# Row sums on VectorE for two parts of the conditioning, with their weights behind the first projection's

## The chip, the cores and the metric

The kernel runs on one core of a Trainium2 chip. The metric is the device time of one execution in microseconds (us), the median of several runs. Engines are named as the profile names them: PE (TensorE, matrix products; PEld its weight loads), DVE (VectorE), ACT (ScalarE), POOL (GpSimd), SP (SyncE, which here only issues DMAs). A time with a start is measured from the start of the span.

## What is computed

One layer for 256 tokens of width 1024. A conditioning vector c is multiplied with a 1024 x 6144 matrix w_ada; the six pieces of 1024 are shifts, scales and gates used in different places. Then two mixers (gated DeltaNet and forgetting attention, "FoX") share one input projection, are gated and merged, and a top-4-of-32 expert network follows.

```python
mod = (c @ w_ada[l] + b_ada[l]).reshape(B, N_MOD, D)
sh1, sc1, gt1, sh2, sc2, gt2 = [mod[:, i, None, :] for i in range(N_MOD)]
h = rms_norm(x, g_norm1[l]) * (1.0 + sc1) + sh1
proj = h @ w_in[l]
# split: dn_qkv, dn_z, dn_b, dn_a, fx_qkv, fx_f, gate_a, gate_b
y_a = o_a.reshape(B, S, DN_W) @ w_o_delta[l]      # DeltaNet branch
y_b = o_b.reshape(B, S, FOX_W) @ w_o_fox[l]       # FoX branch
merged = sigmoid(gate_a) * y_a + sigmoid(gate_b) * y_b
x = x + gt1 * (merged @ w_out[l])
h2 = rms_norm(x, g_norm2[l]) * (1.0 + sc2) + sh2
x = x + gt2 * moe_ffn(h2, ...)
```

All is float32. The change touches c @ w_ada, the order in which weights arrive, and the place of y_b = o_b @ w_o_fox.

## The kernel before

Every engine has its own written-out instruction stream; semaphores join them. SBUF has a ring of 20 slots of 8 KB per partition (1 MB each). Until the experts start, slots 0 to 7 carry a stream of 54 units of 1 MB (list UNITS): unit n goes into slot n mod 8, and SP issues its DMA once unit n - 8 has been used, in order. The order is ada0 (8 units), dn (6), fqk (4), fv (2), z (2), ada1 (8), gates (8), ada2 (8), wo_fox (2), wo_delta (2), w_out (4). The units ada0, ada1 and ada2 are the three parts of w_ada, 2048 columns wide, one unit for each block of 128 rows (k = 0 to 7). Units dn, fqk, fv, z and gates are 256 columns of w_in each. A unit of w_ada is one run of 8 KB per partition, a unit of w_in eight runs of 1 KB.

**Conditioning.** ada(part, b) on PE does four matmuls for each k: block k of c, repeated over 32 columns, is the stationary operand, 512 columns of the unit are the moving one, and the result is summed over k in bank b of PSUM. take_mod_rows on DVE (L1369) copies the bank to mod_rows; mod_transposes on PE (L513 to L520) turns the rows to columns; take_mod on DVE adds the bias. Part 0 is needed for h. Part 1 (gt1, sh2) is done on PE after the products of keys and queries, part 2 (sc2, gt2) inside the DeltaNet recurrence, in three pieces that fill PE's waits (between_state, between_vnew).

**Projection in three passes.** Most units of w_in are split into a rounded half and a rest (list SPLIT): ACT writes the rounded half w_hi to one of three buffers (split_hi, L1096), POOL subtracts and writes the rest w_lo in place over the unit (L1789, two instructions of 128 x 1024 for each unit), and PE takes three products. ACT splits two units ahead of PE; the first two gates units are split after ACT has taken the second z (take, L1130).

**Order of PE around the change.** dn 0 to 5; the small projection; fqk 0 to 2; cumulative sums of the log gates (they need g8 from DVE, L1401 to L1421, a chain of short instructions that also waits for ACT); fqk3, fv, z; chunk_pairs; ada(1) and its transposes; gates 0; six levels of the triangular inverse with half a gates unit between each two steps; the recurrence over four chunks; four blocks of the FoX branch (out_branch with wf and obT, two columns of 128 each); the normalised DeltaNet output transposed (oT_ps), four blocks of its branch; the output projection. DVE's chain after chunk_pairs is: L1482 (scores times decay), L1488 (mask of level 0), L1493, L1488 (level 1), L1499, L1501, and then take_mod_rows(1).

**What follows.** SP issues the first experts' weights on oT_ps, yb_ps, ya_ps, merged_ready and out_ps, as slots come free; then 32 experts stream 12 MB each through the 20 slots.

Of the kernel before, what the change touches and what calls it, by code (L numbers as in the profile page):

```python
# [15 lines left out]
ALU = mybir.AluOpType  # L16
# [3 lines left out]
P = 128  # L20
# [20 lines left out]
def layer_kernel(nc, x, c, w_ada, b_ada, g_norm1, w_in, conv_w, a_log, dt_bias, g_onorm, b_fgate,  # L41
# [3 lines left out]
    KD = D // P  # L45
# [26 lines left out]
    with ExitStack() as ctx:  # L72
# [208 lines left out]
        UNIT_AT = {(name, i): n for n, (name, i, _) in enumerate(UNITS)}  # L281

# [203 lines left out]
        def _(pe):  # L486
# [36 lines left out]
            pe.wait_ge(S("cb_ready"), 1)  # L523
            ada(0, 4, range(2))
# [169 lines left out]
            ada(1, 5)  # L694
# [61 lines left out]
            for h in range(H):  # L756
# [8 lines left out]
            pe.wait_ge(S("hT_whole"), 1)  # L765
            between_state = {1: lambda: project("gates", LEVELS, (1,)), 2: lambda: project("gates", LEVELS + 1, (1,)),
                             3: lambda: ada(2, 6, range(3, 6))}
            between_vnew = {0: lambda: project("gates", LEVELS, (0,)), 1: lambda: project("gates", LEVELS + 1, (0,)),
                            2: lambda: ada(2, 6, range(3)), 3: lambda: ada(2, 6, range(6, KD))}
# [30 lines left out]

            wf = [unit_arrived(pe, "wo_fox", u).rearrange("p (k n) -> p k n", k=2) for u in range(2)]

            def out_branch(w, o, b, g, sem):
                for m in (2 * g, 2 * g + 1):
                    for k in range(H):
                        last = mm(bank(b, (m % 2) * T, T), w[k // 2][:, k % 2, m * P:(m + 1) * P], o[:, k, :],
                                  k == 0, k == H - 1)
                last.then_inc(S(sem), 1)

            pe.wait_ge(S("proj_taken"), nproj[0] - 6)  # L810
            for g in range(4):
                if g >= 2:
                    pe.wait_ge(S("yb_taken"), g - 1)
                out_branch(wf, obT, g % 2, g, "yb_ps")
                if g == 0:
                    mod_transposes(2, 6)
                if g == 1:

                    pe.wait_ge(S("on_ready"), 1)
                    for h in range(H):  # L820
                        for t in range(TT):
                            last = pe.transpose(bank((2, 7)[h // 2], (h % 2) * T + t * P, P), o_sb[:, t, h, :], ident)
                    last.then_inc(S("oT_ps"), 1)
# [231 lines left out]
        def _(act):  # L1055
# [27 lines left out]
            def split_hi(n, m):  # L1083
# [7 lines left out]
                elif prev is not None:  # L1091
                    if m == 0 and name != "fv" and SPLIT[prev][0] != "fv":
                        act.wait_ge(S("half_used"), prev + 1)
                    else:
                        act.wait_ge(S("unit_used"), UNIT_AT[SPLIT[prev]] + 1)
# [17 lines left out]
            def take(name, u):  # L1113
# [9 lines left out]
                act.wait_ge(S("unit_used"), UNIT_AT[(name, u)] + 1)  # L1123
# [206 lines left out]
        def _(dve):  # L1330
# [36 lines left out]
            def take_mod_rows(part, b):  # L1367
                dve.wait_ge(S("unit_used"), UNIT_AT[(f"ada{part}", KD - 1)] + 1)
# [15 lines left out]

            for u in range(6):
                dve.wait_ge(S("unit_used"), UNIT_AT[("dn", u)] + 1)
# [10 lines left out]
                last.then_inc(S("conv_ready"), 1)  # L1397
            dve.wait_ge(S("conv_ready"), 6)
# [9 lines left out]
            STT(ab8, y8, -1.0, y8, ALU.mult, ALU.max).then_inc(S("y8_ready"), 1)  # L1408

# [7 lines left out]
            link(STT(y8, y8, 0.0, g8, ALU.max, ALU.subtract))  # L1417
            dve.wait_ge(S("l8_ready"), 1)
# [18 lines left out]
            last.then_inc(S("rowF_taken"), 1)  # L1437
            dve.wait_ge(S("rowF_taken"), 1)
# [68 lines left out]
            for s in range(1, LEVELS):  # L1507
# [19 lines left out]
                if s == 2:  # L1527
# [6 lines left out]
                    TS(fmax, fmax, -1.0, None, ALU.mult).then_inc(S("fox_max_ready"), 1)  # L1534
                if s == 3:
# [5 lines left out]

            dve.wait_ge(S("M_ready"), LEVELS - 1)
# [3 lines left out]
            for n in range(NCH):  # L1546
                t, r = n // 2, (n % 2) * CH
                rows = slice(r, r + CH)
                if n > 0:
                    dve.wait_ge(S("ws_ps"), n)  # L1550
                    TTn(vnew[rows, t], u_sb[rows, t], ps[rows, 2, :].rearrange("p (h n) -> p h n", h=H),
                        ALU.subtract).then_inc(S("vnew_ready"), 1)
                if n < NCH - 1:
# [7 lines left out]
                    last.then_inc(S("state_ready"), 1)  # L1561
                    dve.wait_ge(S("state_ready"), n + 1)
# [7 lines left out]
            take_yb(0)  # L1570
            take_mod(2, 6)
# [7 lines left out]
            take_yb(1)  # L1579
# [5 lines left out]
            take_yb(2)  # L1585
# [4 lines left out]
            take_yb(3)  # L1590
# [191 lines left out]
        def _(pool):  # L1782
# [9 lines left out]
            pool.wait_ge(S("unit_used"), UNIT_AT[SPLIT[-1]] + 1)  # L1792
# [67 lines left out]
```

## Time and profile before

| | us |
|---|---|
| median of 3 runs (lowest, highest) | 1234.74 (1232.75, 1236.36) |
| the profiled execution's own time | 1238.22 |
| its span, first to last instruction | 1236.4 |
| PE busy | 1140.0 (92%) |
| DVE busy | 318.3 (26%) |
| ACT busy | 185.4 (15%) |
| POOL busy | 106.0 (9%) |
| mean granted TensorE clock | 0.98 of full speed |
| moved by DMA | 464.71 MB, mean 376 GB/s |

How to read the profile: a row of a timeline gives start, duration, engine, line of the kernel and operation, result and operands, shape, how many instructions are merged in it (x), and in brackets how long the engine had been idle and who released it. The duration of an instruction includes time in which it has been issued and is held up. A float32 matmul shows as two instructions. All matmuls go through a helper, so they have line 488 and are told apart by their operands and shapes. "Issue" names a wait for which the profile shows no releaser. The granted clock is the share of TensorE's full speed (2.4 GHz) that it was given; 0.5 is 1.2 GHz.

### The profile page before, as it was taken

The numbers are of one execution on the slowest core, as the hardware profiler recorded it, in microseconds if no ns is written. First come the engines' busy times: TensorE is split into PE (matmuls) and PEld (weight loads), VectorE is DVE, ScalarE is ACT, GpSimd is POOL, SyncE is SP. The second block draws the span as 40 slices with busy tenths as digits, with TensorE's granted clock in tenths as the row PEclk, the third lists the DMA queues.
The fourth block names the chain that finished last, engine by engine and source line by source line (L and its number), as shares of the span: only waits on it lengthen the run. The fifth ranks groups of instructions, "written<-read, shape, count | busy, mean of one in ns | idle before, by whom it ended". The sixth has DMA issues, their size and how long they took to land.

```text
span 1236.4 us, 15127 instructions
## 1 busy us (share of the span) xinstructions
PE 1140.0 (92%) x6307; PEld 588.1 (48%) x6307; DVE 318.3 (26%) x674; ACT 185.4 (15%) x317; POOL 106.0 (9%) x50
## 2 busy tenths in 40 slices
PE   4999999999999999998989998989999999989896
PEld 2999799678543334333334333333433334333332
DVE  1632553131332222212122212121221222122102
ACT  2475344101310000000001000000000010000002
POOL 0764344010000000000000000000000000000000
PEclk9998999999999999999989999999999999999999
DMA  9972773498899999999999999999999999999995
GB/s 351 337 226 93 242 234 103 146 420 335 329 404 426 428 428 428 429 428 429 428 429 428 428 429 428 429 429 428 429 428 429 428 429 428 429 428 428 429 427 246
DMA packets 62559, 464.71 MB, mean 376 GB/s; under 512 B 8469, under 2 KB 31130, under 8 KB 34618
## 3 DMA queue, kind: packets, MB, share of 16 engines
q1 hardware_dynamic: 61688, 462.92, 91.2%
q10 hardware_dynamic: 786, 1.14, 0.3%
q8 instruction: 26, 0.43, 0.1%
q0 software_dynamic: 48, 0.13, 0.0%
q14 instruction: 11, 0.09, 0.0%
HBM read 463.13 MB, written 1.05 MB: 375 GB/s over the span
## 4 chain that ended last, share of the span: by engine, by line
PE 65%; DMA 28%; issue 2%; ACT 2%; DVE 1%; ACTq 0%; POOL 0%; SPq 0%; DVEq 0%
PE ps L488 63%; DMA ring<-in_w_down_dram 16%; DMA ring<-in_w_gate_up_dram 6%; DMA kept<-in_w_down_dram 4%; DMA ring<-in_w_in_dram 1%; PE ps L939 1%; ACT kept L1290 1%; DMA ring<-in_g_onorm_dram 1%; PE ps L971 0%; ACT w_hi L1096 0%; PE ps L496 0%; POOL w_lo L1789 0%; ACT ring L1079 0%; DVE kept L1419 0%; ACT ring L1134 0%
## 5 line engine op out<-in xcount | busy, mean ns | idle before, releaser
L488 PE MATMUL ps<-ring,kept 128*64 128x512 f32 (+1 forms) x3040 | 656.2, 598 | 35.0 <-DMA ring<-in_w_down_dram 19.0
L488 PEld LDWEIGHTS ps<-ring,kept 128*64 128x64 f32 (+1 forms) x3040 | 211.7, 137 | 451.7 <-issue 399.2
L488 PE MATMUL ps<-kept 128*128 128x128 f32 (+4 forms) x984 | 195.7, 415 | 8.3 <-ACT kept L1290 3.3
L488 PEld LDWEIGHTS ps<-kept 128*128 128x128 f32 (+2 forms) x984 | 110.5, 179 | 95.8 <-issue 83.1
L1286 ACT ACTIVATE kept<-kept 128x512 f32<-128x512 f32 x32 | 20.1, 629 | 729.5 <-DVE kept L1691 729.5
L1691 DVE TENSOR_SCALAR kept<-ps 128x512 f32<-128x512 f32 x32 | 22.1, 692 | 384.6 <-PE ps L488 384.6
L1713 DVE TENSOR_TENSOR kept<-ps,kept 64x512 f32<-64x512 f32 x64 | 44.1, 689 | 296.0 <-PE ps L488 295.0
L1789 POOL TENSOR_TENSOR w_lo<-ring,w_hi 128x1024 fp32r<-128x1024 f32 x38 | 91.9, 2434 | 110.3 <-ACT w_hi L1096 110.2
L488 PE MATMUL ps<-hT_hi,w_hi 128*128 128x256 f32 x272 | 78.5, 289 | 0.6 <-POOL w_lo L1789 0.6
L488 PE MATMUL ps<-ring 64*64 64x64 f32 (+6 forms) x784 | 76.0, 272 | 2.9 <-issue 2.9
L488 PE MATMUL ps<-hT_lo,w_hi 128*128 128x256 f32 x272 | 76.8, 282 | 0.0
L488 PE MATMUL ps<-hT_hi,w_lo 128*128 128x256 f32 x272 | 76.8, 282 | 0.0
L488 PEld LDWEIGHTS ps<-ring 64*64 64x64 f32 (+3 forms) x784 | 66.5, 160 | 12.9 <-issue 6.8
L488 PE MATMUL ps<-kept,ring 128*128 128x256 f32 (+1 forms) x252 | 56.2, 380 | 4.5 <-DMA ring<-in_w_in_dram 2.5
L488 PEld LDWEIGHTS ps<-kept,ring 128*128 128x128 f32 x252 | 47.2, 196 | 12.1 <-issue 3.3
L488 PEld LDWEIGHTS ps<-hT_hi,w_hi 128*128 128x128 f32 x272 | 52.1, 191 | 1.3 <-issue 0.8
L488 PEld LDWEIGHTS ps<-hT_lo,w_hi 128*128 128x128 f32 x272 | 52.0, 191 | 0.1
L488 PEld LDWEIGHTS ps<-hT_hi,w_lo 128*128 128x128 f32 x272 | 52.0, 191 | 0.0
L1096 ACT ACTIVATE w_hi<-ring 128x1024 fp32r<-128x1024 f32 x38 | 39.2, 1053 | 49.5 <-PE ps L488 37.5
L939 PE MATMUL ps<-kept 128*128 128x128 f32 x128 | 21.7, 292 | 22.6 <-issue 22.6
L939 PEld LDWEIGHTS ps<-kept 128*128 128x128 f32 x128 | 19.1, 206 | 33.4 <-issue 29.6
L1290 ACT ACTIVATE kept<-ps 128x512 f32<-128x512 f32 x32 | 19.1, 597 | 85.7 <-PE ps L939 85.7
(229 smaller groups left out, 516.4 us busy)
## 6 DMA issues: line engine op xcount, KB each, us to landing
ring<-in_w_gate_up_dram SPq DMA_DIRECT2D x127, 2048.0 KB, 27.8
ring<-in_w_down_dram SPq DMA_DIRECT2D x47, 2048.0 KB, 23.5
kept<-in_w_down_dram SPq DMA_DIRECT2D x16, 2048.0 KB, 25.1
ring<-in_w_ada_dram SPq DMA_DIRECT2D x24, 1024.0 KB, 5.4
ring<-in_w_in_dram SPq DMA_DIRECT2D x22, 1024.0 KB, 11.5
ring<-in_w_out_dram SPq DMA_DIRECT2D x4, 1024.0 KB, 16.2
ring<-in_w_o_fox_dram SPq DMA_DIRECT2D x2, 1024.0 KB, 9.8
ring<-in_w_o_delta_dram SPq DMA_DIRECT2D x2, 1024.0 KB, 12.7
```

The costliest lines, as they stand in the source:

```text
L488: return pe.matmul(dst, lhsT, rhs, start=start, stop=stop, skip_group_check=True)
L939: last = pe.transpose(bank(7, kk * P, P), fours[:, kk, :], ident)
L1096: A(hi_buf_r(n)[:, :, cols], w[:, :, cols], ACT.Copy).then_inc(S("split_hi"), 1)
L1286: A(sig_a, gate_a, ACT.Sigmoid, scale=ALPHA).then_inc(S("sig_ready"), 1)
L1290: A(act_t_last if par == 0 and not more else act_t, bank(7), ACT.Copy).then_inc(S("act_t_ready"), 1)
L1691: TS(gate_a, bank(4), LIMIT, None, ALU.min).then_inc(S("gate_up_taken"), 1)
L1713: TTn(ypair[par * 64:par * 64 + 64, d * 512:(d + 1) * 512], ps[64 * d:64 * d + 64, b, :], gt2_row[64 * d:64 * d + 64, d * 512:(d + 1) * 51 ...
L1789: pool.tensor_tensor(lo_r[:, :, cols], lo[:, :, cols], hi_buf_r(n)[:, :, cols].bitcast(F32), ALU.subtract).then_inc(S("split_lo"), 1)
```

## The change

Parts 1 and 2 of the conditioning are no longer summed over k by PE. DVE multiplies unit k, in place in its ring slot, by the column c of block k and adds the result that it left in the slot of unit k - 1 (add_rows: 8 instructions of 128 x 2048 for a part). PE then sums over the 128 rows with 4 matmuls against a matrix of ones (ada_over_rows). A slot of such a unit comes free when the next sum has read it, or for k = 7 when PE has; SP waits on ada_added and ada_summed for that, and the other units are counted by USED_AT.

The sums are put into DVE's stream at: after convolutions 3, 4 and 5 (part 1, k = 0 to 2), after y8 (k = 3), before the wait for l8 (k = 4), after rowF_taken (k = 5 to 7); behind level 4 (part 2, k = 0 to 2), behind the levels (k = 3), and in the first two recurrence steps (k = 4 to 7).

The units of part 1 move from behind z to places between dn and fv; those of part 2 in part between gates 4 and gates 5; gates 0 and 1 follow z directly. In the recurrence, two blocks of the FoX branch (fox_branch(0), fox_branch(1)) stand where ada(2) had its first two pieces, and ada_over_rows(2) where it had the third. Block 2 follows, then the transposes of part 2, then one column of block 3, the transposes for oT_ps and the other column. DVE's take_yb calls move accordingly.

```diff
@@ the order of the stream
-        UNITS = [("ada0", k, ada_unit(0, k)) for k in range(KD)]
-        UNITS += [("dn", u, win_unit(256 * u)) for u in range(6)]
-        UNITS += [("fqk", u, win_unit(COL_FOX + 256 * u)) for u in range(4)]
-        UNITS += [("fv", u, win_unit(COL_FOX + 2 * W + 256 * u)) for u in range(2)]
-        UNITS += [("z", u, win_unit(COL_Z + 256 * u)) for u in range(2)]
-        UNITS += [("ada1", k, ada_unit(1, k)) for k in range(KD)]
-        UNITS += [("gates", u, win_unit(COL_GATES + 256 * u)) for u in range(8)]
-        UNITS += [("ada2", k, ada_unit(2, k)) for k in range(KD)]
+        UNITS = ada_part(0) + win_part("dn", 0, range(6))
+        UNITS += ada_part(1, (0, 1)) + win_part("fqk", COL_FOX, (0, 1)) + ada_part(1, (2, 3))
+        UNITS += win_part("fqk", COL_FOX, (2,)) + ada_part(1, (4,)) + win_part("fqk", COL_FOX, (3,))
+        UNITS += ada_part(1, (5, 6, 7)) + win_part("fv", COL_FOX + 2 * W, (0, 1)) + win_part("z", COL_Z, (0, 1))
+        UNITS += win_part("gates", COL_GATES, range(5)) + ada_part(2, range(3))
+        UNITS += win_part("gates", COL_GATES, range(5, 8)) + ada_part(2, range(3, KD))
@@ SP
-                    sp.wait_ge(S("unit_used"), n - NSTREAM + 1)
+                    name, i, _ = UNITS[n - NSTREAM]
+                    if name not in SUMMED_NAMES:
+                        sp.wait_ge(S("unit_used"), USED_AT[(name, i)])
+                    elif i < KD - 1:
+                        sp.wait_ge(S("ada_added"), sums_before(int(name[3]), i) + 2)
+                    else:
+                        sp.wait_ge(S("ada_summed"), SUMMED.index(int(name[3])) + 1)
@@ PE
+            def ada_over_rows(part, b):
+
+                pe.wait_ge(S("ada_added"), sums_before(part, KD))
+                w = unit_sb(UNIT_AT[(f"ada{part}", KD - 1)])
+                for q in range(4):
+                    last = mm(ps[32 * q:32 * q + 32, b, :], km("ones")[:, 0:32], w[:, 512 * q:512 * q + 512],
+                              True, True)
+                last.then_inc(S("ada_summed"), 1)
...
-            ada(1, 5)
+            ada_over_rows(1, 5)
...
-                             3: lambda: ada(2, 6, range(3, 6))}
+                             3: lambda: fox_branch(1)}
...
-                            2: lambda: ada(2, 6, range(3)), 3: lambda: ada(2, 6, range(6, KD))}
+                            2: lambda: fox_branch(0), 3: lambda: ada_over_rows(2, 6)}
...
+            pe.wait_ge(S("yb_taken"), 1)
+            fox_branch(2)
+            mod_transposes(2, 6)
+            pe.wait_ge(S("yb_taken"), 2)
...
+            branch_column(wf, obT, 1, 6)
+            pe.wait_ge(S("on_ready"), 1)
+            for h in range(H):
+                for t in range(TT):
+                    last = pe.transpose(bank((2, 7)[h // 2], (h % 2) * T + t * P, P), o_sb[:, t, h, :], ident)
+            last.then_inc(S("oT_ps"), 1)
+            branch_column(wf, obT, 1, 7).then_inc(S("yb_ps"), 1)
@@ DVE
+            def add_rows(part, k):
+
+                n = UNIT_AT[(f"ada{part}", k)]
+                w = unit_sb(n)
+                dve.wait_ge(S(f"slot_in{n % NSTREAM}"), 16 * (n // NSTREAM + 1))
+                if k == 0:
+                    last = TS(w, w, vec("c", k), None, ALU.mult)
+                else:
+                    dve.wait_ge(S("ada_added"), sums_before(part, k))
+                    last = STT(w, w, vec("c", k), unit_sb(UNIT_AT[(f"ada{part}", k - 1)]), ALU.mult, ALU.add)
+                last.then_inc(S("ada_added"), 1)
...
+                if u >= 3:
+                    add_rows(1, u - 3)
...
             STT(ab8, y8, -1.0, y8, ALU.mult, ALU.max).then_inc(S("y8_ready"), 1)
+            add_rows(1, 3)
...
+            add_rows(1, 4)
             dve.wait_ge(S("l8_ready"), 1)
...
+            for k in range(5, KD):
+                add_rows(1, k)
...
+                if s == LEVELS - 2:
+                    for k in range(3):
+                        add_rows(2, k)
...
+            add_rows(2, 3)
...
+                if n < 2:
+                    add_rows(2, 4 + 2 * n)
...
+                    if n < 2:
+                        add_rows(2, 5 + 2 * n)
...
             take_yb(0)
+            take_yb(1)
...
-            take_yb(1)
+            take_yb(2)
```

## Rows read from the trace of the kernel before

**Rows 1.** From the page: shares of the chain that ended last, by engine.

```profile
PE 65%; DMA 28%; issue 2%; ACT 2%; DVE 1%; ACTq 0%; POOL 0%; SPq 0%; DVEq 0%
```

**Rows 2.** Windows: busy us and (instructions) by engine, granted clock, DMA share, GB/s.

```profile
32.00:90.00 58.00, 57.59 (x442) 55.65 (x442) 29.71 (x60) 32.72 (x39) 41.11 (x18) 0.97 0.93 287
...
157.00:247.00 90.00, 90.00 (x955) 78.19 (x954) 31.82 (x39) 31.43 (x68) 26.89 (x12) 1.00 0.47 155
...
321.00:1236.00 915.00, 847.07 (x3946) 331.85 (x3946) 198.37 (x446) 69.81 (x142) 0.00 (x0) 0.99 0.99 421
```

**Rows 3.** Timelines of POOL, DVE and PE before the cumulative sums (g8).

```profile
87.15 4.73 POOL L1789 TENSOR_TENSOR w_lo<-ring,w_hi 128x1024 fp32r<-128x1024 f32 x2 [5.16 <-ACT w_hi L1096]
...
86.15 0.18 DVE L1411 TENSOR_SCALAR kept<-kept 128x16 f32<-128x16 f32 x1 [6.43 <-ACT kept L1151]
...
90.13 1.78 DVE L1419 TENSOR_TENSOR kept<-kept 128x16 f32<-128x16 f32 x1 [2.88 <-ACT kept L1154]
...
92.34 1.71 PE L488 MATMUL ps<-kept,ring 128*128 128x8 f32 x12 [2.07 <-DVE kept L1421]
```

**Rows 4.** Timeline of PE, 137 to 151.5 us: part 1 and its transposes.

```profile
139.34 7.07 PE L488 MATMUL ps<-ring,kept 128*32 128x512 f32 x64
147.66 0.40 PE L513 MATMUL ps<-kept 12*128 12x12 f32 x2 [1.25 <-DVE kept L1369]
```

**Rows 5.** Timelines of PE and ACT, and landings of the wo_fox units' DMAs.

```profile
236.89 2.78 PE L488 MATMUL ps<-ring,kept 128*32 128x512 f32 x24
...
250.15 5.38 PE L488 MATMUL ps<-ring 128*128 128x256 f32 x16 [2.93 <-issue]
...
256.51 3.72 PE L488 MATMUL ps<-ring 128*128 128x256 f32 x16
...
DMA to landing us min/median/max: 8.4/9.8/11.2
...
224.62 0.60 ACT L1130 ACTIVATE ring<-ps 128x512 f32<-128x512 f32 x1 [10.27 <-PE ps L488]
```

**Rows 6.** Timeline of DVE, 136.5 to 151 us: the chain before mod_rows.

```profile
138.53 2.16 DVE L1482 SCALAR_TENSOR_TENSOR ring<-ps,kept,ring 128x128 f32<-128x128 f32 x8 [7.37 <-PE ps L488]
140.72 1.29 DVE L1488 TENSOR_TENSOR ring<-ring 128x512 f32<-128x512 f32 x2
...
146.92 0.68 DVE L1369 COPY kept<-ps 128x512 f32<-128x512 f32 x1
```

**Rows 7.** Timelines of ACT and POOL, same stretch: the split of gates 0.

```profile
137.43 0.60 ACT L1130 ACTIVATE ring<-ps 128x512 f32<-128x512 f32 x1 [5.16 <-PE ps L488]
147.26 2.00 ACT L1096 ACTIVATE w_hi<-ring 128x1024 fp32r<-128x1024 f32 x2 [9.23 <-DMA ring<-in_w_in_dram]
...
148.39 4.73 POOL L1789 TENSOR_TENSOR w_lo<-ring,w_hi 128x1024 fp32r<-128x1024 f32 x2 [18.62 <-ACT w_hi L1096]
```

**Rows 8.** Timelines of POOL and DVE: instructions of both at the same time.

```profile
36.54 16.76 POOL L1789 TENSOR_TENSOR w_lo<-ring,w_hi 128x1024 fp32r<-128x1024 f32 x7 [36.09 <-ACT w_hi L1096]
...
39.10 2.34 DVE L1383 TENSOR_TENSOR wsmall_lo<-ring,wsmall_hi 128x96 fp32r<-128x96 f32 x1
...
170.32 3.51 DVE L1488 TENSOR_TENSOR ring<-ring 128x512 f32<-128x512 f32 x2 [2.56 <-PE ps L488]
...
170.85 2.43 POOL L1789 TENSOR_TENSOR w_lo<-ring,w_hi 128x1024 fp32r<-128x1024 f32 x1 [5.72 <-ACT w_hi L1096]
```

**Rows 9.** Windows, columns as in rows 2: PE after its wait for g8.

```profile
93.70:100.50 6.80, 6.80 (x29) 6.44 (x30) 0.21 (x1) 3.13 (x5) 4.26 (x2) 0.52 0.10 43
```

**Rows 10.** Group of DVE's subtraction; then waits: us in total, times, longest.

```profile
L1380 DVE TENSOR_TENSOR hT_lo<-kept,hT_hi 128x2048 fp32r<-128x2048 f32 x1 | 2.3, 2292 | 2.7 <-ACT hT_hi L1105 2.7
...
DVE ring L1512 <- PE ps L488: 15.0, 5, 7.7
DVE ring L1445 <- ACT ring L1173: 13.5, 1, 13.5
...
DVE ring L1551 <- PE ps L488: 12.3, 3, 5.0
```

More of the change, by code:

```diff
@@ L267, in rows_unit, with ada_part, win_part @@
             return (w[0, r0:r0 + kk * P, :].rearrange("(k p) n -> p k n", p=P), ("p (k n) -> p k n", dict(k=kk)))
[L269 to L276 removed]
+        def ada_part(part, ks=range(KD)):
+            return [(f"ada{part}", k, ada_unit(part, k)) for k in ks]
+        def win_part(name, col, us):
+            return [(name, u, win_unit(col + 256 * u)) for u in us]
+        UNITS = ada_part(0) + win_part("dn", 0, range(6))
[4 more added lines that the diff above has]
+        UNITS += win_part("gates", COL_GATES, range(5, 8)) + ada_part(2, range(3, KD))
         UNITS += [("wo_fox", u, rows_unit(w_o_fox, 256 * u, 2)) for u in range(2)]
@@ L281, in layer_kernel, with sums_before @@
         UNIT_AT = {(name, i): n for n, (name, i, _) in enumerate(UNITS)}
+        SUMMED = (1, 2)
+        SUMMED_NAMES = [f"ada{part}" for part in SUMMED]
+        USED_AT = {}
+        for name, i, _ in UNITS:
+            if name not in SUMMED_NAMES:
+                USED_AT[(name, i)] = len(USED_AT) + 1
+        def sums_before(part, k):
+            return KD * SUMMED.index(part) + k
         WHOLE = 1
@@ L327, in stream @@
                 if n >= NSTREAM:
[L328 removed]
+                    name, i, _ = UNITS[n - NSTREAM]
+                    if name not in SUMMED_NAMES:
+                        sp.wait_ge(S("unit_used"), USED_AT[(name, i)])
[3 more added lines that the diff above has]
+                        sp.wait_ge(S("ada_summed"), SUMMED.index(int(name[3])) + 1)
                 dst = unit_sb(n)
@@ L765, in _, with branch_column, out_branch, fox_branch @@
             pe.wait_ge(S("hT_whole"), 1)
+            def branch_column(w, o, b, m):
+                for k in range(H):
+                    last = mm(bank(b, (m % 2) * T, T), w[k // 2][:, k % 2, m * P:(m + 1) * P], o[:, k, :],
+                              k == 0, k == H - 1)
+                return last
+            def out_branch(w, o, b, g, sem):
+                for m in (2 * g, 2 * g + 1):
+                    last = branch_column(w, o, b, m)
+                last.then_inc(S(sem), 1)
+            def fox_branch(g):
+                wf = [unit_arrived(pe, "wo_fox", u).rearrange("p (k n) -> p k n", k=2) for u in range(2)]
+                if g < 2:
+                    pe.wait_ge(S("proj_taken"), nproj[0] - 7 + g)
+                out_branch(wf, obT, g % 2, g, "yb_ps")
             between_state = {1: lambda: project("gates", LEVELS, (1,)), 2: lambda: project("gates", LEVELS + 1, (1,)),
-                             3: lambda: ada(2, 6, range(3, 6))}
+                             3: lambda: fox_branch(1)}
             between_vnew = {0: lambda: project("gates", LEVELS, (0,)), 1: lambda: project("gates", LEVELS + 1, (0,)),
-                            2: lambda: ada(2, 6, range(3)), 3: lambda: ada(2, 6, range(6, KD))}
+                            2: lambda: fox_branch(0), 3: lambda: ada_over_rows(2, 6)}
             for n in range(NCH):
@@ L1367, in take_mod_rows @@
             def take_mod_rows(part, b):
-                dve.wait_ge(S("unit_used"), UNIT_AT[(f"ada{part}", KD - 1)] + 1)
+                if part in SUMMED:
+                    dve.wait_ge(S("ada_summed"), SUMMED.index(part) + 1)
+                else:
+                    dve.wait_ge(S("unit_used"), USED_AT[(f"ada{part}", KD - 1)])
                 CP(mod_rows, bank(b)).then_inc(S("mod_rows_sb"), 1)
@@ L1584, in _ @@
             last.then_inc(S("oaT_ready"), 1)
-            take_yb(2)
+            take_yb(3)
             TTn(wrout, wrout, A2.unsqueeze(2).to_broadcast([P, KD, E]), ALU.mult)
```

29 lines of the change are left out of this document (5 added, 24 removed).

## Prediction

> **What bounds the kernel now.** I read the chain of work first [rows 1]: PE holds 65% of it and DMA 28%. The stages tell these apart [rows 2]. From 321 us on, the DMA engines are 99% busy at 421 GB/s: the experts' weights stream, and that stage lasts as long as its bytes. It starts when the mixers' output lets the last ring slots go, so what the stages before it gain or lose moves the end by as much. Between 157 and 247 us PE is busy 90.00 of 90 us: there PE's own work sets the end and nothing else. Outside that stretch PE has a few short waits, and the rows name them: 2.07 us on VectorE before 92.34 [rows 3], 1.25 us on VectorE before 147.66 [rows 4], 2.93 us before 250.15 [rows 5]. The last is put down to "issue", but it is a DMA: the two wo_fox units are issued only when slots of the third conditioning part come free, and take up to 11.2 us to land [rows 5].
>
> **The change, part by part.**
>
> *Matmuls taken away.* A conditioning part is 32 matmuls with 32 columns, shown as 64 instructions: 7.07 us [rows 4]. Three of eight row blocks of the third part are 2.78 us, so that part is 7.4 [rows 5]. Afterwards each part is 4 matmuls, an eighth: 0.9 us. PE loses 12.7 us of work. What that gains has to be read at the two places.
>
> *Second part, 137 to 151 us.* After its 7.07 us PE does not go on: it waits 1.25 us more, because the transposes at 147.66 need mod_rows, which VectorE copies from 146.92 to 147.60, at the end of a chain that began at 138.53 [rows 4, 6]. That chain is there before and after; the matmuls only ran beside it. So the 6.2 us taken from PE here become idle time, from 140.2 to 147.7. All that the place can give is the 0.6 us for which gates 0, whose weights land late, holds PE at 150.3 (my reading of when its first subtraction ends, 148.39 + 2.37 [rows 7]).
>
> *What the earlier stream sets free.* Before, the split of gates 0 and 1 (ACT rounds, POOL subtracts) starts at 147.26, when the unit has landed; ACT had been idle 9.23 us for it and POOL 18.62 us [rows 7]. In the new order gates 0 and 1 follow z; their slots come free with fqk3 and with sums of the second part, all over by about 110 us, so they lie in SBUF long before 138. ACT then splits right after it has taken z1 at 137.43 [rows 7], and POOL's four subtractions, 2.37 us each, run from about 139.1 on, exactly over VectorE's chain. Do they collide? The trace shows it [rows 8]: a VectorE TENSOR_TENSOR of 96 elements took 2.34 us while POOL ran seven subtractions back to back, and at 170.32 a pair that takes 1.29 us alone [rows 6] took 3.51, its second half waiting for POOL's instruction of 170.85 to end. Each waits for a whole instruction of the other, and they take turns. In the chain, L1488, L1493 and again L1488 (two each, the pair of rows 6 three times) and L1501 have both inputs in SBUF; L1482, L1499 and the mod_rows copy read PSUM, and I leave them their length. With turns: subtraction 1 to 141.45, L1488a 142.0, subtraction 2 144.4, L1488b 144.95, subtraction 3 147.35, L1493a 147.9, subtraction 4 150.3, L1493b 150.85. The rest, 4.2 us (from two pairs after 140.72 to 147.60), is free of POOL: mod_rows at 155.1, 7.5 us late, and PE idles 15 us. The trace prices what idleness does to the clock: after the 2.07 us the granted clock was 0.52 from 93.7 to 100.5, the level of 1.2 GHz, a loss of half of 6.8 us, 3.4 [rows 9]; after the 2.93 us sixteen instructions took 5.38 in place of 3.72, a loss of 1.7 [rows 5]. I take 2.5. The place costs 7.5 - 0.6 + 2.5 = 9.4 us (8.5 to 11).
>
> The Trainium skill (SBUF — State Buffer, section "Who interferes with whom") states the same for VectorE instructions with two SBUF inputs against a GpSimd instruction that reads SBUF, and that the loser waits for the whole instruction. That speaks against this change: by it the new sums, of which no row here shows the like beside a POOL instruction, take turns too. Without the rule the place would cost 1.9 us, and the sums nothing.
>
> *The sums of the second part.* A sum reads two SBUF operands of 2048 elements: 2.29 us by the subtraction of that shape [rows 10]; the first of each part has one operand, and lies between half of that and the whole. Three come after convolutions 3, 4 and 5. They keep the port from POOL for up to 6.9 us, but POOL is busy only 41 of the 58 us there [rows 2] and works more than a half unit ahead of PE: nothing. The one after y8 (k = 3) lies in VectorE's 6.43 us wait for ACT that ends at 86.15 [rows 3]: nothing. The next (k = 4) has no room. It asks just after POOL has taken the port at 87.15 for the first of two subtractions; it gets it at 89.5 and keeps it to 91.8; POOL's second takes its turn to 94.2; and L1419, which ended at 91.9, ends at 94.3 [rows 3]. g8 comes 2.4 us later, and PE waits for exactly that. It starts at 94.7 with the clock already low: by 100.5 it has done 2.9 us of full-speed work in place of 1.4 + 3.4 = 4.8, a loss of 1.9, and more if the low stretch goes on (2.4 + 1.7 = 4.1 at most). I take 2.5. If fv0's split is ready by 94.2 too, POOL slips in twice more and g8 is 7 us late. fv0 is issued when the k = 3 sum has ended (79.7, one turn, the sum: about 85); gates 0, issued when the first ada1 unit was used (139.34 + 7.07/8 = 140.2), was with ACT at 147.26, 7 us later, and an ada unit is ahead of fv0: 92 to 94, which is close. The last three sums, 6.9 us, fit in VectorE's 13.5 us before L1445 [rows 10].
>
> *The sums of the third part.* Three behind level 4, up to 6.9 us, fit in the 7.7 us before L1512 [rows 10], but hold back POOL's last subtraction until PE just misses it: 0.3. The one behind the loop and four in the recurrence, 2.29 each in gaps of up to 5.0 us with no subtractions left [rows 10], are hidden. If that cover were gone, each would cost its 2.29.
>
> *The tail, from 236.89 us.* Removed: 7.4 of matmuls, 2.93 of waiting for wo_fox (its second unit is now issued when gates 6 is used, by 224.62, and wanted at 236.9 [rows 5]: 12 us for a landing of 8.4 to 11.2), and 1.66 of low clock behind that wait. Together 12.0. Added: 0.9 for the four matmuls; 1.4 of waiting for yb_taken, which VectorE gives only after copying mod_rows (0.7) and take_yb (0.7); about 0.5 for on_ready, which stands behind mod_cols in VectorE's queue. The fox blocks that move forward keep their length. Gain 12.0 - 2.8 = 9.2. The experts' first DMAs wait on oT_ps, yb_ps and out_ps, which move with PE.
>
> **Sum**: 2.5 + 9.4 + 0.3 - 9.2 = +3.0 us. The profiled run took 1238.22 us with a span of 1236.4; it would take 1241.2. On the median of 1234.74 that gives **1237.7 us**. A measurement of this kernel can tell about 0.3% from no change, 3.7 us: 1231.0 to 1238.4. The forecast lies inside, near the upper end.
>
> **The rivals.**
>
> *A, faster: no collision in the pair stage.* If POOL's subtractions do not hold up the chain (other turns, or gates 0 landing late after all), mod_rows comes at 147.6 and the place costs the clock's 2.5 less 0.6. Then 2.5 + 1.9 + 0.3 - 9.2 = -4.5, and about -7 if g8 is spared for the same reason: 1228 to 1230. For it: the pair of rows 8 lost only one turn. Against it: seven instructions that need the port must pass four subtractions, and any order of turns that I lay out ends between +6.5 and +7.5.
>
> *B, slower: g8 caught twice.* If fv0's split is ready before L1419 ends, L1420 and L1421 wait for one more subtraction each. PE loses 6.5 instead of 2.5: +7.0, 1241.7. It decides at one point, fv0 landing before 93.2.
>
> *C: the sums take no turns with POOL.* g8 stays where it is: +0.5, 1235.2.
>
> *D: the tail does not give*, because wo_fox's slots still come late, behind sums that are late: half of the gain gone, about +7.5, 1242.
>
> **Chances.** Forecast 0.50, A 0.20, B 0.15, C 0.10, D 0.05. The forecast spreads by about 2.5 us with the clock, so two fifths of it lie over 1238.4. Slower: 0.20 + 0.15 + 0.05 = 0.40. Faster: A, 0.20. Same: 0.40. The range takes in A and B, 1228 to 1243; the forecast's own is 1235 to 1241.
>
> **What would show it.** Right: PE idle from about 142 to 157 us, ended by the mod_rows copy; L1488 and L1493 there at twice their length or more; POOL's four subtractions starting within 2 us of ACT's taking of z1; L1419 about 2.4 us later; no wait of PE for wo_fox. Wrong: those pairs at 1.29 us, or POOL idle until the chain is over (A); a wait before g8 over 6 us (B), or under 2.5 (C); a wait on in_w_o_fox (D). An experts' stage of another length would overturn the assumption that shifts carry through.

## The result and the profile after

The changed kernel took 1243.93 us (median of 4 runs, 1243.65 to 1244.47) where the kernel before took 1233.74 beside it: ratio 1.0075 with a 95% interval of 1.0060 to 1.0091, so 9.3 us more on the 1234.74 of the table, 1244.0. A second set of runs gave 1245.60 against 1234.03, ratio 1.0088 (1.0075 to 1.0101). The change makes the kernel slower, by 7.4 to 11.2 us in the first set and by 9.3 to 12.5 us in the second. The forecast said 1237.7 with a range of 1228 to 1243: the sign of its sum was right, its size (3.0 us) a third of what came, and the measured time lies 1 us above the range and 3 us above the 1241 that was the forecast's own upper end.

The profiled execution of after took 1243.7 us with a span of 1241.5, that of before 1238.22 with 1236.4. The traces differ by 5.1 us and the medians by 9.2, because the profiled execution of before stands near the top of its own runs: all others lay between 1232.2 and 1238.5, with medians of 1233.7 to 1235.0. So the steps below account for the 5.1, and the rest is dealt with at the end.

The chain's shares, with columns as in rows 1. DVE was 1% and is 3%:

```profile
PE 65%; DMA 27%; DVE 3%; issue 2%; ACT 2%; ACTq 0%; SPq 0%; DVEq 0%
```

PE's waits between 20 and 345 us (what waited, for whom; us in total, times, longest):

```profile
PE ps L532 <- DVE kept L1407: 14.1, 1, 14.1
PE ps L507 <- DVE kept L1475: 6.2, 1, 6.2
...
PE ps L507 <- DVE ring L1632: 1.5, 1, 1.5
```

The first is the wait for mod_rows, 1.25 before [rows 4]. The second is the wait for g8, 2.07 before [rows 3]. The third is the new wait for yb_taken. The 2.93 for wo_fox [rows 5] is gone.

**g8.** Timelines of DVE, POOL, ACT and PE (start, us, engine, line, operation, count, idle before and what ended it), and two windows with columns as in rows 2:

```profile
87.22 4.42 DVE L1432 SCALAR_TENSOR_TENSOR ring<-ring,kept 128x2048 f32<-128x2048 f32 x1
91.56 2.32 DVE L1473 TENSOR_TENSOR kept<-kept 128x16 f32<-128x16 f32 x1
93.92 2.26 DVE L1474 SCALAR_TENSOR_TENSOR kept<-kept 128x8 f32<-128x8 f32 x1
96.10 0.16 DVE L1475 TENSOR_SCALAR kept<-kept 128x8 f32<-128x8 f32 x1
96.30 3.26 DVE L1478 COPY ring<-kept 128x2048 f32<-128x2048 f32 x1
...
87.08 11.38 POOL L1853 TENSOR_TENSOR w_lo<-ring,w_hi 128x1024 fp32r<-128x1024 f32 x4 [5.16 <-ACT w_hi L1131]
...
92.41 2.00 ACT L1131 ACTIVATE w_hi<-ring 128x1024 fp32r<-128x1024 f32 x2 [0.56 <-DMA ring<-in_w_in_dram]
...
96.41 0.78 PE L507 MATMUL ps<-kept,ring 128*128 128x8 f32 x3 [6.20 <-DVE kept L1475]
...
93.70:100.50 6.80, 4.02 (x18) 3.95 (x19) 6.00 (x5) 2.48 (x3) 4.77 (x3) 0.50 0.88 292
100.50:104.00 3.50, 3.50 (x18) 3.38 (x18) 0.00 (x0) 0.57 (x1) 0.00 (x0) 0.54 0.00 0
```

L1432 is the k = 4 sum. It waited for POOL's first subtraction, then POOL's second and L1473 took turns, as forecast (sum to 91.64, L1473 to 93.88; forecast 91.8 and 94.3). But fv0 landed at 92.4, its first subtraction was ready, and L1474, an instruction of 8 elements, waited for it too: 2.26 us. g8 came at 96.3 instead of 92.3.

**The pair stage.** The same views, 141 to 166 us:

```profile
142.91 2.16 DVE L1538 SCALAR_TENSOR_TENSOR ring<-ps,kept,ring 128x128 f32<-128x128 f32 x8 [7.37 <-PE ps L507]
145.11 4.00 DVE L1544 TENSOR_TENSOR ring<-ring 128x512 f32<-128x512 f32 x2
149.15 5.46 DVE L1549 TENSOR_TENSOR ring<-kept,ring 128x512 f32<-128x512 f32 x2
154.64 1.29 DVE L1544 TENSOR_TENSOR ring<-ring 128x512 f32<-128x512 f32 x2
...
158.18 0.68 DVE L1407 COPY kept<-ps 128x512 f32<-128x512 f32 x1
...
142.31 3.88 ACT L1131 ACTIVATE w_hi<-ring 128x1024 fp32r<-128x1024 f32 x4
...
143.44 10.62 POOL L1853 TENSOR_TENSOR w_lo<-ring,w_hi 128x1024 fp32r<-128x1024 f32 x4 [9.26 <-ACT w_hi L1131]
...
158.92 0.41 PE L532 MATMUL ps<-kept 12*128 12x12 f32 x2 [14.12 <-DVE kept L1407]
...
148.40:158.80 10.40, 0.00 (x0) 0.00 (x0) 10.33 (x9) 0.00 (x0) 5.66 (x3) 0.50 1.06 399
158.92:165.20 6.28, 6.28 (x30) 5.80 (x31) 1.72 (x5) 0.00 (x0) 0.00 (x0) 0.50 0.14 57
```

Against rows 6: the first two pairs take 4.00 and 5.46 where each takes 1.29 alone, while POOL's four subtractions run from 143.44 to 154.06; the third pair, after them, takes 1.29 again. From the chain's start to mod_rows it is 15.95 us instead of 9.07. POOL's four took 10.62 where two took 4.73 [rows 7], so both sides pay. The last window shows PE with work and the clock at 0.50, the 1.2 GHz level, for 6.3 us more.

**The tail.** PE's timeline, then the DMA issues of wo_fox (last column: median us from issue to landing), then ACT's first and last activation of one kind in the experts' stage:

```profile
259.81 1.06 PE L507 MATMUL ps<-ring,kept 128*32 128x512 f32 x8
262.41 3.72 PE L507 MATMUL ps<-ring 128*128 128x256 f32 x16 [1.54 <-DVE ring L1632]
...
ring<-in_w_o_fox_dram SPq DMA_DIRECT2D x2, 1024.0 KB, 6.0
...
346.52 0.63 ACT L1321 ACTIVATE kept<-kept 128x512 f32<-128x512 f32 x1 [14.54 <-DVE kept L1755]
...
1211.78 0.63 ACT L1321 ACTIVATE kept<-kept 128x512 f32<-128x512 f32 x1 [15.67 <-DVE kept L1755]
```

The fox blocks run at full length, and wo_fox lands in 6.0 us without a wait. The two marks of the experts' stage are 865.26 us apart; in the trace of before they stand at 341.99 and 1207.26, 865.27 apart. In this pair the shift is carried through the stage unchanged. The equality to 0.01 us is luck: over the fourteen traces of all the kernels here, the same two marks are 863.5 to 866.0 us apart.

### The profile page after: what moved, and what is told of

Read it like the earlier page. It is cut to its first block, busy times and chain, and to the rows that moved or that the text cites. A ratio compares the mean times of both kernels' runs of the same rounds, so it can differ in the third digit from the quotient of the medians.

```text
span 1241.5 us, 14934 instructions
## 1 busy us (share of the span) xinstructions
PE 1131.6 (91%) x6195; PEld 586.6 (47%) x6195; DVE 373.8 (30%) x690; ACT 185.4 (15%) x317; POOL 113.3 (9%) x50
## 4 chain that ended last, share of the span: by engine, by line
PE 65%; DMA 27%; DVE 3%; issue 2%; ACT 2%; ACTq 0%; SPq 0%; DVEq 0%
PE ps L507 62%; DMA ring<-in_w_down_dram 16%; DMA ring<-in_w_gate_up_dram 6%; DMA kept<-in_w_down_dram 4%; PE ps L974 1%; ACT kept L1325 1%; DMA ring<-in_w_in_dram 1%; DMA ring<-in_g_onorm_dram 1%; DVE ring L1549 0%; DVE ring L1544 0%; DVE ring L1432 0%; PE ps L1006 0%; PE ps L515 0%; DVE ring L1478 0%; DVE kept L1474 0%
## 5 line engine op out<-in xcount | busy, mean ns | idle before, releaser
L507 PE MATMUL ps<-ring,kept 128*64 128x512 f32 (+2 forms) x2928 | 642.7, 597 | 33.1 <-DMA ring<-in_w_down_dram 19.0
L507 PEld LDWEIGHTS ps<-ring,kept 128*64 128x64 f32 (+2 forms) x2928 | 208.2, 138 | 441.8 <-issue 393.1
L507 PE MATMUL ps<-kept 128*128 128x128 f32 (+4 forms) x984 | 199.0, 422 | 8.3 <-ACT kept L1325 3.3
L1853 POOL TENSOR_TENSOR w_lo<-ring,w_hi 128x1024 fp32r<-128x1024 f32 x38 | 98.2, 2605 | 116.7 <-ACT w_hi L1131 116.7
L1432 DVE SCALAR_TENSOR_TENSOR ring<-ring,kept 128x2048 f32<-128x2048 f32 x14 | 42.3, 3024 | 1.4 <-ACT ring L1252 0.5
```

What stands on the lines that cost most here:

```text
L507: return pe.matmul(dst, lhsT, rhs, start=start, stop=stop, skip_group_check=True)
L1432: last = STT(w, w, vec("c", k), unit_sb(UNIT_AT[(f"ada{part}", k - 1)]), ALU.mult, ALU.add)
L1853: pool.tensor_tensor(lo_r[:, :, cols], lo[:, :, cols], hi_buf_r(n)[:, :, cols].bitcast(F32), ALU.subtract).then_inc(S("split_lo"), 1)
```

## The experiments

The theory: two collisions of VectorE with POOL's subtractions (before g8, and over the pair chain) cost some 14 us, and the tail gives 8 back. The rivals: the sums themselves or the changed order of the stream cost the time, or the clock does so alone.

**1. The k = 4 sum moved behind the cumulative sums.**

```diff
-            add_rows(1, 4)
             dve.wait_ge(S("l8_ready"), 1)
...
             dve.wait_ge(S("cums_taken"), 1)
+            add_rows(1, 4)
```

> The changed kernel with one sum moved: the k = 4 sum of part 1 stands behind cums_taken, not inside the g8 chain. Theory (turns at the port): the chain L1473 to L1475 is no longer caught three times, g8 comes about 4 us earlier, PE's wait for it falls from 6.2 to about 2 us and the whole run from 1243.9 to about 1239.5. Rival (PE is late there because units arrive late, or the sum's own length is what counts and merely moves): no change, 1243.9, or worse, since fv1's slot comes free later.

Measured 1238.18 (1235.1 to 1239.5), 5.7 below after by the medians and 5.3 by the ratios to before (1.0032 against 1.0075). PE's wait for g8 is 2.1 us again, L1472 (the same instruction as L1419 in rows 3) is back at 90.13, and the wait for mod_rows is 14.1 as in after. The place of one sum costs some 5.5 us although the sum is hidden in itself.

```profile
90.13 1.77 DVE L1472 TENSOR_TENSOR kept<-kept 128x16 f32<-128x16 f32 x1 [2.88 <-ACT kept L1189]
```

**2. ACT splits gates 0 and 1 only after mod_rows.**

```diff
+            act.wait_ge(S("mod_rows_sb"), 2)
             for n in range(BEFORE_GATES, BEFORE_GATES + 2):
                 split_hi(n, 0)
```

> The changed kernel with ACT's split of gates 0 and 1 held back until mod_rows has been copied, so that POOL has nothing to do during VectorE's chain. Theory: the chain takes 9.1 us again instead of 15.9, PE's wait before the transposes falls from 14.1 to about 7 us; PE then waits some 1 us for the first subtraction of gates 0. Net 5 to 7 us faster than the changed kernel: about 1238. Rival (the chain is long for another reason, for example the low clock or the DMA traffic of that moment): the wait stays at 14 us and the run gets slower by the later split, 1246.

Measured 1237.87 (1235.9 to 1239.1), 6.1 below after. DVE's and POOL's timelines:

```profile
145.52 1.29 DVE L1545 TENSOR_TENSOR ring<-ring 128x512 f32<-128x512 f32 x2
146.85 1.29 DVE L1550 TENSOR_TENSOR ring<-kept,ring 128x512 f32<-128x512 f32 x2
148.18 1.29 DVE L1545 TENSOR_TENSOR ring<-ring 128x512 f32<-128x512 f32 x2
...
151.72 0.68 DVE L1408 COPY kept<-ps 128x512 f32<-128x512 f32 x1
...
153.58 4.70 POOL L1854 TENSOR_TENSOR w_lo<-ring,w_hi 128x1024 fp32r<-128x1024 f32 x2 [18.98 <-ACT w_hi L1131]
```

Every pair is back at 1.29 and PE waits 7.3 us, which is the chain of before with nothing beside it. The split of two units started later is cheaper than the same split started early at the wrong moment.

**3. Both at once.** Edits 1 and 2 together.

> The change with both corrections at once: the k = 4 sum behind the cumulative sums (as in the run that moved it), and ACT's split of gates 0 and 1 behind the mod_rows copy (as in the run that delayed it). Alone they gave 5.7 and 6.1 us. If the change's +9 us is these two stalls and nothing beside them, the gains add: 1243.9 - 11.8 = 1232. If the two share something (the whole change costs 3.5 us more than its two halves measured alone, 1227.2 and 1247.8), the sum is missed: what the second half alone gives, 1227.2, plus what is left in the pair stage with a free chain (PE idle for 7 us there, clock low behind it, less 0.6 for gates 0: about 2), so 1229. PE's waits should be about 2 us for g8 and 7 us for mod_rows.

Measured 1231.46 (9 runs, 1230.0 to 1233.0), with 1245.60 for the whole change beside it and ratio 0.9979 (0.9969 to 0.9988) to before. That is 14.1 below the whole change measured beside it, and 12.5 below its first median; single gains of 5.7 and 6.1 add to 11.8. PE's waits are 7.2 and 2.1. So the two stalls are all of the loss: every sum and every unit of the stream is still in its new order, and the kernel is 2.6 us faster than before. The clock cannot be held apart from the stalls, since its low stretches shrink with them: in half-microsecond windows it is low from 95.5 to 99.0 and from 143.0 to 154.0, where a second trace of the whole change has 96.5 to 107.0 and 151.0 to 168.5. Of the two ways of reckoning in the expectation, 12 off the whole change gives 1233.8 beside this measurement, 2 on top of the second half 1229.6 + 2 = 1231.6. The median is the second, and all nine runs lie below the first. But the gains of 5.7 and 6.1 were measured on another chip, from runs that spread over 3 to 4 us, so this does not decide between them.

**4. The second half alone**: sums for the third part and the new tail; the second part on PE and its units behind z, as before.

```diff
-        SUMMED = (1, 2)
+        SUMMED = (2,)
...
-            ada_over_rows(1, 5)
+            ada(1, 5)
...
-            add_rows(1, 3)
...
-            add_rows(1, 4)
```

> Only the third part summed on VectorE, with the tail of the changed kernel; the second part, its units in the stream and its matmuls as in the kernel before. Theory: the tail gives 8.4 us and nothing is lost before it, so 8 us faster than the kernel before: about 1226. Rival (the tail's gain is eaten in the experts' stage, since the changed kernel is 9 us slower in time although its trace is late by only 4.5): faster by less than 4 us, 1231 or more.

> The second half alone (third part's sums, their order in the stream and the tail), again: -7.9 us in the other call. If the halves add, it and the first half give the whole's difference.

Measured 1227.16 with 1235.04 for before, ratio 0.9941 (0.9923 to 0.9960), and again 1229.64 with 1234.03 (1225.3 to 1231.4), ratio 0.9960 (0.9945 to 0.9976). The half makes the kernel 4 to 8 us faster; the second set lies between the theory's 1226 and the rival's 1231. The windows behind g8 of its first trace show the clock back at full speed by 97.5, where before (same code up to there) stays low until 100.5 [rows 9]. The last line is the second trace of the same half, which stays low as before does:

```profile
93.70:97.50 3.80, 3.80 (x21) 3.80 (x21) 0.21 (x1) 2.10 (x3) 3.80 (x2) 0.55 0.24 101
97.50:100.50 3.00, 3.00 (x21) 2.77 (x20) 0.00 (x0) 1.25 (x2) 0.70 (x1) 1.00 0.02 5
...
93.70:100.50 6.80, 6.80 (x31) 6.44 (x31) 0.42 (x2) 3.58 (x5) 4.72 (x2) 0.51 0.17 71
```

Nine of the fourteen traces have this wait of 2.07 us. In five the low clock behind it lasted some 3.5 us and cost 1.7, in four (before is one) it lasted some 7 and cost 3.4.

**5. The first half alone**: the second part's sums and its place in the stream; third part and tail as before.

```diff
-        SUMMED = (1, 2)
+        SUMMED = (1,)
...
-                            2: lambda: fox_branch(0), 3: lambda: ada_over_rows(2, 6)}
+                            2: lambda: ada(2, 6, range(3)), 3: lambda: ada(2, 6, range(6, KD))}
```

> Only the second part summed on VectorE, with its units behind dn in the stream; the third part and the tail as in the kernel before. Theory: g8 and the pair stage cost what they cost in the changed kernel (about 4.5 to 6 and 8.4 us), the tail gives nothing: 13 to 16 us slower than the kernel before, 1248 to 1251. Together with e3 (7.9 us faster) the two halves should add up to the whole change, +9 us. Rival (the two halves interact, for example in the stream's order or the experts' stage): their sum misses the whole by more than 4 us.

> The first half alone (second part's sums and their place in the stream), again: +12.8 us in the other call. The trace of the whole change shows +14.3 for these two places, so if the effects add this half should stand 14 to 17 above before, and if the shortfall is real 12 to 13.5.

Measured 1247.80 with 1234.10 for before, ratio 1.0104 (1.0087 to 1.0121), and again 1245.17 with 1234.03, ratio 1.0091 (1.0078 to 1.0104). The half cost less than the 13 to 16 and the 14 to 17 that adding up the trace's places had given. By the medians the halves give -7.9 and +13.7 at first, -4.4 and +11.1 the second time, together 5.8 and 6.7, while the whole change gives 10.2 and 11.6: 4 to 5 us are missing, also the second time, where all three ran on one chip. So the effects of the halves do not add. Three of it can be read in the traces. PE's timeline at wo_fox in the two traces of this half, to be laid beside rows 5:

```profile
262.61 3.69 PE L506 MATMUL ps<-ring 128*128 128x256 f32 x16 [1.65 <-issue]
```

```profile
263.43 3.69 PE L506 MATMUL ps<-ring 128*128 128x256 f32 x16 [1.88 <-issue]
```

Before, PE waited 2.93 us there and the block behind took 5.38 at the low clock. With the first half the wait is 1.65 or 1.88 and the clock stays up: the block takes 3.69. That is 1.3 + 1.7 = 3.0 us (2.7 in the other). The first half gets these microseconds, the second half also gets them when it is alone, and the whole change gets them once. The 1 to 2 us that remain are within what runs of one kernel differ by.

**6. Nothing but the collision, in the kernel before.** Four subtractions of 128 x 1024 on POOL into a tile that nothing reads at that time, released when the pairs' matmuls end. No sums, and the stream as before.

```diff
+                if n == BEFORE_GATES:
+                    pool.wait_ge(S("pairs_ps"), 1)
+                    for j in range(4):
+                        pool.tensor_tensor(xg, ..., ALU.subtract).then_inc(S("filler"), 1)
+                        pool.wait_ge(S("filler"), j + 1)
```

> The kernel before with nothing of the change, but four extra POOL subtractions of 128 x 1024 (of data nobody uses) released by pairs_ps, so that they run beside VectorE's chain from L1482 to the mod_rows copy. Theory (turns at the port): the chain is 6.5 to 7.5 us longer, PE waits about 8 us before its transposes instead of 1.25, and the run is 7 to 9 us slower than the kernel before: about 1243. Rival (POOL does not hold up the chain; it is the idle PE or the order of units that costs): chain unchanged, PE only waits for gates 0's later subtraction, at most 3 us slower.

Measured 1247.29, ratio 1.0101 (1.0080 to 1.0121), 12.3 us more. DVE's and POOL's timelines:

```profile
140.39 3.56 DVE L1488 TENSOR_TENSOR ring<-ring 128x512 f32<-128x512 f32 x2
143.99 5.50 DVE L1493 TENSOR_TENSOR ring<-kept,ring 128x512 f32<-128x512 f32 x2
149.53 5.47 DVE L1488 TENSOR_TENSOR ring<-ring 128x512 f32<-128x512 f32 x2
...
138.24 10.70 POOL L1787 TENSOR_TENSOR kept<-kept 128x1024 f32<-128x1024 f32 x4 [8.78 <-PE ps L488]
149.02 11.47 POOL L1795 TENSOR_TENSOR w_lo<-ring,w_hi 128x1024 fp32r<-128x1024 f32 x4
```

The first two pairs take 3.56 and 5.50 us, for 4.00 and 5.46 in after, with none of the change's sums present: the collision alone makes the delay. The size was expected at 7 to 9 and is larger for a reason the edit brought: the four real subtractions of gates 0 and 1 queue behind the four fillers, at 149.02, and catch the third pair too.

**7. Two mends of the pair stage.** Both keep the whole change with the k = 4 sum moved (edit 1). The mod_rows copy goes right behind L1538, PE does gates 0 ahead of part 1's transposes, and the two take_yb calls go ahead of the third part's mod_rows copy. The second version also lets ACT split gates 1 only after it has taken gates 0.

```diff
             ada_over_rows(1, 5)
+            project("gates", 0)
             mod_transposes(1, 6)
...
+            take_mod_rows(1, 5)
             link(last)
...
-            for n in range(BEFORE_GATES, BEFORE_GATES + 2):
-                split_hi(n, 0)
-                split_hi(n, 1)
+            split_hi(BEFORE_GATES, 0)
+            split_hi(BEFORE_GATES, 1)
             take("gates", 0)
+            split_hi(BEFORE_GATES + 1, 0)
+            split_hi(BEFORE_GATES + 1, 1)
```

> The changed kernel with the k = 4 sum behind cums_taken, mod_rows copied right after L1482 instead of at the chain's end, PE's gates 0 ahead of the transposes of part 1, and in the tail two take_yb before the copy of part 2's mod_rows. Theory: PE has 5.8 us of gates 0 to do while VectorE and POOL take turns, then waits only for X1 (near 151): the stage ends at about 153.5 where it ended at 156.7 before, and with the tail's 8.4 + 1.5 us the run is 12 to 13 us faster than the kernel before: 1222. Rival (PE then waits as long for the first subtraction of gates 0 and for X1): 1226 or more.

> As b1_gates_first, and ACT splits gates 1 only after it has taken gates 0, so that two of POOL's four subtractions run beside the chain instead of four. Theory (each subtraction beside the chain costs one turn of 2.4 us): X1 comes 4 to 5 us earlier than in b1, the stage ends about 2 us earlier, 1220. Rival (what matters is the total of POOL's work, not its place): same as b1, or slower by the later subtraction of gates 1.

The first measured 1230.29, ratio 0.9961 (0.9943 to 0.9979); five of its six runs lie between 1229.5 and 1231.1, one at 1224.4. Its expectation was 1222; the rival's bound (1226 or more) held. PE now had work over the first part of the chain, but the collision was still there and the wait came back one step later, on the copy of U1 that stands behind the whole chain in DVE's queue:

```profile
PE ps L507 <- DVE ring L1562: 4.4, 1, 4.4
```

The second measured **1224.47** (1223.7 to 1225.3), ratio 0.9921 (0.9904 to 0.9938): 9.6 us under before, 19.5 under the change's first median. Two subtractions lie over the chain instead of four, and only the first pair is held:

```profile
139.56 3.57 DVE L1546 TENSOR_TENSOR ring<-ring 128x512 f32<-128x512 f32 x2
143.17 1.29 DVE L1551 TENSOR_TENSOR ring<-kept,ring 128x512 f32<-128x512 f32 x2
...
137.42 5.17 POOL L1853 TENSOR_TENSOR w_lo<-ring,w_hi 128x1024 fp32r<-128x1024 f32 x2 [9.26 <-ACT w_hi L1131]
147.57 5.08 POOL L1853 TENSOR_TENSOR w_lo<-ring,w_hi 128x1024 fp32r<-128x1024 f32 x2 [4.99 <-ACT w_hi L1131]
```

I had put 2 us on that step and it gave 5.8 (though 1224.5 is still above the 1220 expected, since the first version missed by more). The traces show of what: PE's wait on the U1 copy fell from 4.4 to 1.7 us, and the low clock behind it, which the first version had for 10.5 us with 6.1 of work in them, did not come. Windows of the first version, then the second:

```profile
150.00:160.50 10.50, 6.13 (x31) 5.84 (x29) 5.66 (x11) 1.08 (x2) 0.00 (x0) 0.51 0.72 271
...
150.00:160.50 10.50, 10.38 (x104) 10.01 (x105) 4.52 (x5) 2.14 (x3) 5.02 (x3) 1.00 0.69 257
```

The first version bundles four edits; two of them were measured alone (experiments 1 and 8), the mod_rows copy and the place of gates 0 were not. The second differs from the first in ACT's split only.

**8. take_yb ahead of mod_rows, in the second half alone.**

```diff
-            take_mod_rows(2, 6)
...
             take_yb(0)
             take_yb(1)
+            take_mod_rows(2, 6)
```

> As e3_part2_only, with two take_yb ahead of the copy of part 2's mod_rows on VectorE. Theory: PE's wait of 1.5 us for yb_taken before the third fox block goes, the rest stays: 1225.7 against 1227.2. Rival: the wait only moves behind mod_cols (take_yb was not what held it), 1227.

Measured 1225.37 (1223.8 to 1229.3), ratio 0.9934 (0.9912 to 0.9955). That is 1.8 under the first median of the second half and 4.3 under its second, but the intervals of the ratios overlap, so the times alone do not show a gain. The trace does: PE's wait of 1.54 us for yb_taken is gone, and from the four matmuls of the third part to the transposes of the DeltaNet output it is 8.02 us instead of 9.80. The forecast's 1.4 was about the right price of that wait.

## Why the prediction was right or wrong

The mechanism of the forecast was right where most of its sum stood, in the pair stage and the tail. Two steps failed: L1474 was taken as free in the g8 chain, and a difference between traces was put on a median as if the trace were a usual one.

**What bounds the kernel**: held. PE ends everything up to the experts. That stage took 865.3 us in both traces, but it is a constant only to the 2.5 us by which the fourteen traces differ in it.

**g8, +2.5 forecast, +4.4 in the trace.** From here comes the first miss. The beginning of the next chain moved from 138.53 [rows 6] to 142.91. The turns up to L1473 came as laid out to 0.4 us. The step that failed is that L1474 was taken as free. The landing of fv0 was not the error: 92.4 lies in the 92 to 94 that I gave, but also before the 93.2 that rival B named as its point. B's mechanism is what happened, by half: L1474 was caught, L1475, with one input, was not. B had this place at 6.5, since it let both be caught; its sign, a wait before g8 of over 6 us, is there with 6.20. The low clock lasted 10.2 us instead of 6.8 [rows 9], which is inside the 4.4. Experiment 1 prices the place at 5.3 to 5.7 in whole runs. I should have weighed B higher: its condition was called close, and it got 0.15.

**Pair stage, +9.4 forecast, +8.4 in the trace.** The mechanism and nearly the size were right. The chain became 6.9 us longer (forecast 7.5), gates 0 end 12.8 us later where the chain began 4.4 later, which leaves 8.4; with the 0.6 that was no longer waited for gates 0, the low clock cost 2.1 (forecast 2.5). The order of turns was the one laid out: the second pair paid two subtractions, the third pair and L1501 none. Rival A, no collision, is refuted by experiments 2 and 6 together: without the overlap the pairs take 1.29, and with the overlap alone they take 3.6 to 5.5. The Trainium skill (SBUF — State Buffer, section "Who interferes with whom") says that a VectorE instruction with two SBUF inputs and one of GpSimd that reads SBUF exclude each other. Experiment 6 agrees, with 3.56 us against 1.29.

**That the sums take turns** held, and rival C fell. The k = 4 sum took 4.42 us beside POOL; the sum at 218.70 us, with POOL idle for most of it, took 2.35. The gb copy, of one SBUF input, took 3.26 us beside POOL and 1.23 in experiment 1. The same section of the Trainium skill lists copies among the instructions that can take the shared port; the 3.26 agrees with it, and I had not applied it to this row.

**Sums behind level 4, +0.3 forecast.** The recurrence starts 12.83 us later, gates 0 had ended 12.82 later, so the term is about zero. One instruction was held up, without effect on PE, by the third sum:

```profile
210.73 6.80 DVE L1432 SCALAR_TENSOR_TENSOR ring<-ring,kept 128x2048 f32<-128x2048 f32 x2 [0.46 <-DVE ring L1429]
217.46 1.21 DVE L1568 TENSOR_TENSOR ring<-ring,ps 128x1024 f32<-128x1024 f32 x1
```

**The tail, -9.2 forecast, -8.3 in the trace.** At the next stage behind it the shift is 4.5 us where it had been 12.8. The wait for wo_fox and its low clock went as said (rival D is refuted by the absence of any wait on it). Of the 0.9 that are missing, yb_taken has 0.14 (1.54 for 1.4) and the four matmuls 0.16 (1.06 for 0.9); on_ready cost 0.53 for 0.5, and I cannot place the rest.

**The sum.** In the trace 4.4 + 8.4 + 0.0 - 8.3 = 4.5; the experts' stage begins 4.5 us later, and the span is 5.1 longer, 0.6 of it behind the last mark. Against the forecast of 3.0 that is 2.1 us of miss: +1.9 from g8, -1.0 from the pair stage, -0.3 from the levels, +0.9 from the tail and +0.6 at the end. That the misses of g8 and of the pair stage have opposite signs was luck.

**From the trace to the median.** The other 4 us were lost in the step "on the median of 1234.74 that gives 1237.7". I added a difference against a profiled execution of 1238.22 to a median of 1234.74. That execution was 3.5 us slower than the kernel's median, while the one of after (1243.7) stands at its own (1243.93). The other traces show what the same stretches of code usually take. The stretches are: from the start to the pair chain (L1482 or its like), from there to the end of gates 0 on PE, and from there to the first mark of the experts' stage. Code as before stands in before and in experiments 4, 6 and 8 for the first, without 6 for the second, in before and 6 for the third; code as after in both traces of the whole change and in experiments 2 and 5 for the first, without 2 for the second, in the whole change alone for the third.

| stretch | code as before, us | code as after, us | difference | in the two traces of the forecast |
|---|---|---|---|---|
| to the pair chain | 137.08 to 138.97, median of 5: 138.20 | 142.91 to 145.37, median of 5: 143.73 | +5.5 | +4.4 |
| to the end of gates 0 | 17.35 to 18.87, median of 4: 17.8 | 26.63 to 26.93, median of 4: 26.8 | +9.0 | +8.4 |
| to the experts' mark | 185.27 and 183.46 | 176.98 and 176.76 | -7.5 | -8.3 |

Together that is 7.0 where the two traces gave 4.5: 2.5 of the 4 us. Part of it is the clock behind g8: before's trace was one of the four with the long low stretch, while all five traces with the 6.2 us wait have one of some 10 us. The last 1.5 us stay open. My range had no allowance for the 2 us by which traces of one kernel differ without any edit (142.91 and 145.37 for the whole change, 137.08 and 138.97 for the second half).

## What to carry to other kernels

Work moved off the bounding engine brings nothing where a chain on another engine ends at the same place; what then counts is what the freed data and buffers start earlier. Two engines that hold each other up are to be scheduled against each other: before moving a large instruction on VectorE, or making GpSimd's input early, look for the other engine's timeline at that moment, and for the small instruction on the critical path behind it. Where halves of a change go different ways, measure them apart: here one half lost 11 to 14 us and the other won 4 to 8, and an order of the same work in which fewer of these instructions meet turned 9 us slower into 10 us faster.

## What the runs showed of the hardware that was not expected

- An instruction's size does not protect it: L1474, 128 x 8 elements and 0.17 us alone (experiment 1), took 2.26 us, nearly one whole subtraction of POOL (2.37).
- With both queues full, the turns go instruction by instruction even where VectorE's follow each other without a gap: a pair of 1.29 us alone took 3.56 to 4.00 us (2.3 to 2.7 more, about one subtraction of POOL), or 5.46 to 5.50 (4.2 more, nearly two).
- The stretch at 1.2 GHz behind a wait is not fixed by the wait: after 2.07 us it lasted some 3.5 us in five executions and some 7 in four, after 6.20 us some 10 in all five, and around the 14.12 us wait it ran from 148.4 to 165.2, 6.3 us of which PE had work. After a wait of 1.65 or 1.88 us at wo_fox it did not come at all, after 2.93 us (before) and 2.75 us (experiment 6) in the same place it did.
- Repeated runs of the second half spread over 6 us (1225.3 to 1231.4), those of before over as much in all (1232.2 to 1238.5): a change worth 4 us needs more than one profile on each side.
